# The expert table turned by VectorE in squares of 32 instead of by TensorE, and 32 instead of 64 tokens served by gathered rows

## The reference

```
q = (tb @ w_q).reshape(nt, PEER_HEADS, 2, PEER_DK)
sc = jnp.einsum('thcd,hcnd->thcn', q, keys).astype(jnp.float32)
s1, i1 = lax.top_k(sc[:, :, 0], PEER_TOPK)
s2, i2 = lax.top_k(sc[:, :, 1], PEER_TOPK)
...
top_s, j = lax.top_k(cand_s, PEER_TOPK)
eid = jnp.take_along_axis(cand_i, j, axis=-1)
g = jax.nn.softmax(top_s, axis=-1)
act = jax.nn.gelu(jnp.einsum('thkd,td->thk', u[eid], tb).astype(jnp.float32), approximate=False)
return jnp.einsum('thk,thkd->td', (g * act).astype(v.dtype), v[eid])
```

## Time and profile before

| | us |
|---|---|
| median of 3 runs | 3649.49 (3648.81 to 3653.74) |
| the profiled execution | 3645.04 |
| its span in the trace | 3643.2 |
| PE busy | 3373.2 (93%) |
| DVE, ACT, POOL busy | 1736.0, 1467.0, 1059.1 |
| start of `peer`, first and last matmul of `hidden` | 1909.3, 1928.5, 2909.2 |
| output stage | 2913.9 to the end |

### The profile page before, as it was taken

How to read it: one execution, slowest core, us unless ns; L and a number is a source line. 1 busy time by engine, 2 the same in 40 slices (tenths; PEclk the granted TensorE clock), 3 DMA queues, 4 the chain that set the end, 5 groups by cost and what they waited for, 6 DMA issues and landing times. The chain is left out here.

```text
span 3643.2 us, 58753 instructions
## 1 busy us (share of the span) xinstructions
PE 3373.2 (93%) x23240; PEld 3097.5 (85%) x23240; DVE 1736.0 (48%) x2388; ACT 1467.0 (40%) x2057; POOL 1059.1 (29%) x763
## 2 busy tenths in 40 slices
PE   7999997968889786799799999999999899999998
PEld 7999996748878776799799999999999877777776
DVE  5344443432210002464437645565554477777764
ACT  5333222114512233442426666565565433333332
POOL 0000000005513343000106775666668711111100
PEclk9999997659988797899899999999999999999999
DMA  6544443325443532566434447888888798889874
GB/s 202 186 161 161 161 162 98 98 95 159 145 169 120 195 106 68 191 200 197 130 123 155 158 163 246 313 287 286 313 277 310 291 367 309 314 313 331 312 239 158
DMA packets 397704, 753.22 MB, mean 207 GB/s; under 512 B 57149, under 2 KB 334941, under 8 KB 347454
## 3 DMA queue, kind: packets, MB, share of 16 engines
q1 hardware_dynamic: 375838, 610.44, 49.9%
q0 software_dynamic: 18432, 134.23, 9.9%
q10 hardware_dynamic: 3264, 6.29, 0.5%
HBM read 690.86 MB, written 59.51 MB: 206 GB/s over the span
## 5 line engine op out<-in xcount | busy, mean ns | idle before, releaser
L2425 POOL TENSOR_TENSOR peer_uT_low<-peer_uT,peer_uT_high 128x512 fp32r<-128x512 f32 x420 | 555.1, 1352 | 393.1 <-ACT peer_uT_high L2463 387.6
L944 POOL TENSOR_TENSOR gate_low<-gate_raw,gate_high 128x512 fp32r<-128x512 f32 x192 | 245.0, 1300 | 1162.6 <-ACT gate_high L900 1162.4
L2306 PE MATMUL banks<-x_high,peer_uT_high 128*128 128x224 f32 x2048 | 473.4, 280 | 0.0
L2307 PE MATMUL banks<-x_low,peer_uT_high 128*128 128x224 f32 x2048 | 463.7, 274 | 0.0
L2307 PEld LDWEIGHTS banks<-x_low,peer_uT_high 128*128 128x128 f32 x2048 | 393.2, 192 | 0.0
L2306 PEld LDWEIGHTS banks<-x_high,peer_uT_high 128*128 128x128 f32 x2048 | 393.1, 192 | 0.0
L227 PE MATMUL banks<-x_high,win_high 128*128 128x288 f32 (+1 forms) x1312 | 349.1, 296 | 0.0
L228 PE MATMUL banks<-x_low,win_high 128*128 128x288 f32 (+1 forms) x1312 | 348.7, 295 | 0.0
L2463 ACT ACTIVATE peer_uT_high<-banks 128x512 fp32r<-128x512 f32 x512 | 306.7, 629 | 0.0
L197 ACT ACTIVATE win_high<-win_raw 128x2048 fp32r<-128x2048 f32 x84 | 160.8, 1915 | 334.2 <-DVEq L190 329.0
L2434 POOL DMA_INDIRECT peer_area<-in_peer_v_dram,peer_expert_row x64 | 136.1, 2127 | 462.3 <-DVE peer_area L2651 449.1
(11 more groups left out here) (385 smaller groups left out, 7385.4 us busy)
## 6 DMA issues: line engine op xcount, KB each, us to landing
peer_u<-in_peer_u_dram SPq DMA_DIRECT2D x128, 1024.0 KB, 5.2
win_raw<-in_w_in_dram SPq DMA_DIRECT2D x38, 2048.0 KB, 8.1
peer_area<-in_peer_v_dram SPq DMA_DIRECT2D x64, 1024.0 KB, 5.9
peer_u<-in_peer_v_dram SPq DMA_DIRECT2D x64, 1024.0 KB, 5.7
gate_raw<-in_w_in_dram SPq DMA_DIRECT2D x96, 512.0 KB, 4.1
w_raw<-in_w_up_ret_dram SPq DMA_DIRECT2D x8, 2048.0 KB, 9.1
w_raw<-in_w_out_dram SPq DMA_DIRECT2D x8, 2048.0 KB, 8.1
w_raw<-in_peer_w_q_dram SPq DMA_DIRECT2D x8, 2048.0 KB, 8.1
```

Source lines behind the costliest of these rows:

```text
L944: pool.tensor_tensor(self.low[:, p % 2, c, :, :], self.raw[:, p % 4, :, c * P:(c + 1) * P], self.high[:, p % 2, c, :, :], ALU.subtract).th ...
L2306: pe.matmul(out, UH[:, c, k, :], XH[:, k, 0:DENSE], start=(k == 0), stop=False)
L2307: pe.matmul(out, UH[:, c, k, :], XL[:, k, 0:DENSE], start=False, stop=False)
L2425: pool.tensor_tensor(UL[:, m % 2, 4 * b:4 * b + 4, :], UT[:, 4 * b:4 * b + 4, :], UH[:, m % 2, 4 * b:4 * b + 4, :], ALU.subtract).then_inc ...
```

## The change

- **Turning.** SP loads a block of `peer_u` in four DMAs, one per quadrant of 32 partitions: partition 32g+e gets, of the four experts 32E+e, the quarter g of the row, 2 KB each. DVE then transposes squares of 32x32 (`turn`, two instructions a block, each 128 partitions x 1024 elements) straight into `UT`, which now has two slots. The elements of a row of the model so lie in another order over the partitions, and everything that is multiplied with it must have that order: `peer_w_q` is loaded by quadrants too (`QuadrantWeightStream`), hT is copied within SBUF by 16 DMAs (`move_rows`) while `output_projection` runs, and the gain is loaded in four.
- **Halves.** ACT rounds each block in two instructions of 128x1024 from SBUF, POOL subtracts the whole block in two. PE no longer turns anything, and `low_quarter` is gone from DVE.
- **Order on DVE.** The transposes of 64 blocks are dealt out among the instructions of the top 16s by weights that stand in a table (`worked`: 40, 44 and 44 halves for the three tiles).
- **Tokens.** SPARSE is 32, so DENSE 256: 48 matmuls of 256 columns a block, 64 groups of four tokens to spread, weights of 4 MB for every 64 tokens, SHARES 4, SLOTS 32: 32 gathers and dots on `peer_u`, 32 gathers and sums on `peer_v`.
- **Spreading** starts at block 67 and runs in ten of every 14 blocks, one or two groups a block. SECOND is now made by ACT (`second`: four instructions of 128x128 and one of 128x512 a group), FIRST stays on DVE.
- **Dots** run from half 52 to half 248 (6 up to half 130, then 26), all sums in the output stage. Scores of a tile come in one piece.

The diff, cut to its core:

```diff
-SPARSE = 64
+SPARSE = 32
+def by_quadrant(rows):
+    return rows.rearrange("(g c i) n -> g i c n", g=4, i=32)
+class QuadrantWeightStream(WeightStream):
+    def load(self, sp, i, b, columns, first=False):
...
+        for g in range(4):
+            sp.dma_start(self.raw[32 * g:32 * g + 32, b, :, :], columns[g]).then_inc(self.loaded[b], 16)
+def move_rows(sp, area, hT, g, moved):
+    by_row = area[:, A_QT:A_QT + KT * T].rearrange("p (r q t) -> p q r t", q=4, t=T)
+    for q in range(4):
+        sp.dma_start(by_row[32 * g:32 * g + 32, q, :, :], hT[32 * q:32 * q + 32, 4 * g:4 * g + 4, :]).then_inc(moved, 16)
# output_projection, SP
+                    if i >= 2:
+                        sp.wait_ge(w.bank_free, after(2 + 4 * (i - 1)))
+                        move_rows(sp, area, hT, i - 2, moved)
...
+                sp.wait_ge(w.bank_free, after(2 + 16))
+                move_rows(sp, area, hT, 3, moved)
# ffn_norm, DVE
+                dve.wait_ge(moved, after(256))
# peer
+PICK_WEIGHTS = (3, 4, 30)
+PICK_HALVES = (40, 44, 44)
+SPREAD_FROM, SPREAD_ACTIVE, SPREAD_SPAN = 67, 10, 14
+DOTS = ((52, 130, SLOTS * 3 // 16), (130, 248, SLOTS - SLOTS // 8 if SPARSE > NEW else SLOTS))
...
                 def load_u(m):
-                    sp.wait_ge(turned, after(4 * (m - 2) + 4))
-                    sp.dma_start(U[:, m % 2, :], u_in[m]).then_inc(u_loaded[m % 2], 16)
+                    sp.wait_ge(turned, after(2 * (m - 2) + 2))
+                    for g in range(4):
+                        sp.dma_start(U_PARTS[32 * g:32 * g + 32, m % 2, :, :], u_in[g, m]).then_inc(u_loaded[m % 4], 16)
...
# POOL
+                def low_halves(m):
+                    for b in range(2):
+                        pool.wait_ge(uT_high, after(2 * m + b + 1))
+                        if b == 0:
+                            pool.wait_ge(hidden_done, after(m - 1))
+                        part = slice(b * HALF, (b + 1) * HALF)
+                        pool.tensor_tensor(UL[:, m % 2, part, :], UT[:, m % 2, part, :], UH[:, m % 2, part, :], ALU.subtract).then_inc(low, 1)
# ACT
+                        act.activation(UH[:, m % 2, part, :], UT[:, m % 2, part, :], ACT.Copy).then_inc(uT_high, 1)
+                def second(q):
+                    act.wait_ge(placed, after(q - 1))
+                    for j in range(4):
+                        ins = act.activation(SECOND[:, b, j, :], iota[:], ACT.Abs, bias=SEL[:, 1, t:t + 1], scale=-1.0)
+                    act.wait_ge(distances, after(q + 1))
+                    act.activation(SECOND[:, b, :, :], SECOND[:, b, :, :], ACT.Relu, bias=1.0, scale=-1.0).then_inc(second_ready, 1)
# DVE
+                def turn(h):
+                    m, b = divmod(h, 2)
+                    if b == 0:
+                        dve.wait_ge(u_loaded[m % 4], after(64 * (m // 4) + 64))
+                    dve.wait_ge(low, after(2 * (m - 2) + b + 1))
+                    cols = slice(b * HALF * 32, (b + 1) * HALF * 32)
+                    dve.transpose(UT[:, m % 2, b * HALF:(b + 1) * HALF, :].rearrange("p c (E e) -> p E c e", E=4),
+                                  U_PARTS[:, m % 2, :, cols].rearrange("p E (c i) -> p E c i", i=32)).then_inc(turned, 1)
+                def worked(t, weight):
+                    work[0] += weight
+                    while work[1] < PICK_HALVES[t] * work[0] // PICK_TOTAL:
+                        work[1] += 1
+                        half_block()
```

## The result

The changed kernel takes 3626.47 us (median of 4 runs, 3625.30 to 3631.06) where the kernel before takes 3650.99 (4 runs): ratio 0.9933, 95% interval 0.9918 to 0.9948. It is faster, but by 24.5 us, and not by the 148 that the prediction had; the time lies above the range from 3452 to 3612 that it gave eight in ten.

The account below looks back on a forecast made before the run. PE, busy 93% of the span, was taken as the bound: 3645.0 - 199 (PE work, idle, start) + 14 (picks) + 31 (spread) + 1.5 + 4.6 = 3497, or 3501 us as median; eight in ten from 3452 to 3612.

Parts of the forecast that it names:

- rival A: DVE transposes in the picks run at half the pace, 2.3 us a half; time 3610; chance 0.08.
- B: Rival: quadrant loads of U run at half the old rate, 6.1 us a block; time about 3609; chance 0.12.
- C: Rival: DMA sets the hidden stage and the kernel gets slower, about 3745 at 7.0 us a block of U; chance 0.10.
- The start: Start of the hidden stage: U loaded and turned beside keys and scores, scores in one piece; 7 us gained.
- the folds: Three folds instead of one, on DVE in series, SP waiting for the last before loading `HT`: 4.6 us more.
- four FIRST of 0.36 for 1.14 groups 1.6: DVE in the spread: `FIRST` costs 1.6 of 5.1 us a block, which fits.
- rival E: POOL and DVE lock one another out: POOL 7.7 us in active blocks, 6.1 in picks; time about 3530; chance 0.16.
- blocks 0 to 63 at 5.87: Picks of the hidden stage: 5.87 us a block instead of PE's 5.65, 14 us more.
- the 57 blocks of the spread at 7.2: Blocks 67 to 123: 7.2 us each, between PE's 6.67 and DMA's 7.6, close to ACT's; 31 us more.
- on average 7.0 us: ACT's work a block in the spread, 7.6 us in active blocks, against PE's average 6.67.
- Before `peer`: `move_rows` hidden by `output_projection` except its last four issues: 1.5 us more.
- Rival D: Everything hides and PE never waits; time 3456; chance 0.12.

Follow-up runs that it names:

- e6: Changed kernel with e5's two edits and U loaded by plain rows (hidden values wrong, same work): 3500.47 us, ratio 0.9577.
- e2: Changed kernel with U loaded by plain rows, 128 partitions in one transfer (hidden values wrong, same work): 3556.86 us, ratio 0.9742.
- e3: Changed kernel with `FIRST` reading its row of numbers from PSUM, not SBUF: 3567.56 us, ratio 0.9766.
- e10: e6 with the six wide comparisons of the picks reading their 16 numbers from PSUM: 3499.96 us, ratio 0.9576.
- e14: e10 with the six dots moved out of the picks and three quarters of each dot's second input from PSUM: 3483.61 us, ratio 0.9532.
- e5: Changed kernel with GELU store in front of the load of U and `FIRST` from PSUM: 3570.54 us, ratio 0.9776.
- e12: e5 with quadrants 2, 3 of U issued from ACT, wide comparisons from PSUM, six dots moved behind block 65: 3532.35 us, ratio 0.9664.
- e11: Kernel before with only SPARSE changed from 64 to 32, TensorE still turning U: 3693.10 us, ratio 1.0116.
- e16: e12 with the stores of W issued by ACT on its queue, two blocks earlier: 3532.47 us, ratio 0.9665.

## Why the prediction was wrong

**Right: the sizes.** A block on PE is 5.65 us wherever PE is let:

```profile
2002.20 2.05 PE L2327 MATMUL banks<-x_high,peer_uT_low 128*128 128x256 f32 x16
2007.85 2.04 PE L2327 MATMUL banks<-x_high,peer_uT_low 128*128 128x256 f32 x16
```

A transpose is 1.233 us in the median (1.21 forecast), so rival A falls. `low` has a median of 2.41 us and a mean of 2.65 in the picks (2.35 alone). DVE in e6, where it seldom waits for loads, works 363.95 us on 64.1 blocks, 5.7 a block (5.6 to 5.9 forecast). DMA in the changed kernel's picks works 0.87 x 400 us on 61.2 blocks, 5.7 a block (5.5 forecast), and quadrants cost 1.8 us a block more than plain rows (0.88 x 6.50 - 0.62 x 6.24), where 2.1 were forecast. So rivals B and C fall as sums: the share is 0.82 to 0.87, not near 1. The place that they named is nonetheless the dearest one found, 70 us by e2. The start is 12.7 us (19.2 before; 7 gained forecast, 6.5 measured), and from the last low product to the end it is 738.9 us, 4.9 more than before (4.6 forecast, the folds).

**Wrong: `FIRST`** was put at 0.36 us, "four FIRST of 0.36 for 1.14 groups 1.6", from the earlier trace rows, where POOL's `low` came in pieces of 1.29 us. The change makes them 2.35, two in a row, and DVE's `FIRST` goes to a mean of 876 ns from 2435 to 2735 us. e3: 61 us. The prediction saw the lock for wide instructions in the earlier trace rows and had rival E for it, but E spread the locked time evenly over POOL and gave 3530. What happened is a delay of DVE, at one place, with PE's spread and the next transpose behind it.

**Wrong: the busiest engine's load taken for the pace, and the loads of U at no cost.** The steps "blocks 0 to 63 at 5.87" and "the 57 blocks of the spread at 7.2" took for the pace the load of the busiest engine, or a mean of two. The quadrant loads cost nothing in the picks by this reckoning, since 5.5 us of DMA are under 5.65; e2 puts them at 70 us in all. What the runs show in its place is that most blocks go at PE's own time and a few stand for long at one place. In the picks of e10 DVE works 363 us on 64.8 blocks, 5.6 a block, and still 56 of 64 blocks take PE's 5.65: the two with the picks hold 21 of the 27 us above PE's own work. In e14, without these dots, 60 of 64 do, and the picks go at 5.86, of which 5.76 is PE's own work with the scores. In the spread of e5 DMA's work is 0.95 x 7.60, 7.2 us a block, over PE's 6.65, and still 45 of 56 blocks take PE's own time; five blocks, all where one quarter of the tokens follows the other, hold 47 of the 53 us above it. So the near equal loads as such cost little here. What costs is a long instruction, or a queue of transfers, in front of something short that PE waits for, and a sum of loads has no term for it.

**Missing: the clock.** There was no term for it, since before it was at its lower level once in the stage, for 6.8 us, behind the wait of 7.9 us of the earlier trace rows. In the changed kernel there are 18 such spells, of 3.4 to 10.2 us, and each begins behind or in idle time of PE. Here PE waits 3.1 us for the picks; from its second matmul on the starts are 0.12 us apart four times, and then 0.21 us:

```profile
2222.21 0.38 PE L2322 MATMUL banks<-x_high,peer_uT_high 128*128 128x256 f32 x1 [3.11 <-ACT peer_picks_T L2474]
2222.42 0.28 PE L2323 MATMUL banks<-x_low,peer_uT_high 128*128 128x256 f32 x1
...
2222.90 0.41 PE L2323 MATMUL banks<-x_low,peer_uT_high 128*128 128x256 f32 x1
2223.10 0.41 PE L2322 MATMUL banks<-x_high,peer_uT_high 128*128 128x256 f32 x1
2223.32 0.41 PE L2323 MATMUL banks<-x_low,peer_uT_high 128*128 128x256 f32 x1
```

The granted clock (the number behind POOL's) was 1.00 before and during the wait, 0.50 behind it, which is 1.2 in place of 2.4 GHz, and then 1.00 again:

```profile
2217.00:2222.00 5.00, 2.10 (x19) 1.86 (x17) 5.00 (x25) 2.65 (x4) 5.00 (x3) 1.00 0.45 116
2223.00:2226.00 3.00, 3.00 (x16) 3.00 (x16) 2.51 (x12) 0.00 (x0) 3.00 (x2) 0.50 1.04 219
2227.00:2232.00 5.00, 5.00 (x45) 5.00 (x44) 3.81 (x15) 2.28 (x3) 0.90 (x1) 1.00 0.96 204
```

PE was busy for 76 us at this level, so 38 us were lost in this way beside 110 us of idle time. In other runs it was a quarter to four tenths of the idle time: 5 us on 21 in e14, 8 on 34 in e6, 20 on 57 in e12, 29 on 67 in e3.

**Wrong, but without weight:** ACT was "on average 7.0 us" a block, from figures that give 6.1 (7.6 in ten blocks, 2.5 in four); in e6 it is busy 273 of 400 us, 4.8 a block, and bounds nothing. Before `peer`, 12.3 us more and not 1.5: 9.2 of them are there before `output_projection`, in code that both kernels have. That is how much executions differ: over the traces of all runs that stage starts between 1661.1 and 1675.1 us, at 1662.0 in that of the kernel before, and at 1670.2 in e11, whose code is the same up to there. The other 3 us come from there to `peer`, where `move_rows` stands.

Together: 118 us in the stage, 11 before it, 0.3 behind it, for 129 on the scale of the profiled executions. e6, without the locked `FIRST` and the quadrant loads, comes to 3500, but the prediction's 3501 is no better for it, since it counted those loads in. Rival D, at 3456, was never reached; e14 comes nearest with 3484.

**A better kernel.** e12 computes all that the reference asks for, in 3532 us: 3.4% less than the kernel before and 2.7% less than the changed one. e16 is its equal.

## What to carry to other kernels

When a change takes work off the bounding engine and leaves three others within a few per cent of it, don't take the busiest one's load as the pace: look, in order on each engine, for the longest instruction that can hold up a short one, and read the times of single blocks, not their mean. Count PE's idle time about a third as much again for the clock, as here (38 us on 110). Making instructions longer to have fewer of them is paid by whoever shares a port with them; and taking one instruction off the port can hand its wait to the next. And the largest share of the chain is a suspect, not a price: here it was worth 14 of 125 us.

## What the hardware did that I had not expected

- An instruction of DVE that waits for the port pair does not get it at the next gap: a dot waited through the rest of one `low` and two more, 5.7 us, while POOL ran them one after the other (7.08 us for three).
- One operand in PSUM frees an instruction of DVE from POOL: 128x128 then took 0.065 us more in the median (402 ns for 337) and 411 ns at the most, 128x2048 took 2272 ns, as against 2292 at the least from SBUF. The multiplications with two inputs from SBUF right behind the latter then took 3.5 and 3.9 us.
- With loads of U into 32 partitions the DMA engines moved 230 GB/s of their busy time on one queue or dealt out as 0, 2 and 1, 3, 262 with the halves of the partitions on two queues, and 344 with loads into 128 partitions by 8 KB (all transfers of the picks).
- Behind 3.1 us of waiting PE's granted clock was 0.50 for 3.4 us, and over the stage such spells cost 38 us beside 110 of idle time.
